# One identity for all stages, last stores moved between queues, last keys turned from features, and weights waited for one by one

## The reference

```python
xp = layer_norm(x_prompt, ln_in_g, ln_in_b)              # xs likewise for the 64 sample rows
q, k, v, z, xbc, dt_raw, u, vc = split_cols(x @ w_in, IN_SIZES)
o_a = band_attention_prompt(q, k, v, attn_rel_bias)      # 6 heads x 64, a band of 9 chunks of 64
k_rows, v_rows = k[:, L - keep:], v[:, L - keep:]        # returned: the last 512 keys and values
...                                                      # (sample: attention on cache_k, cache_v; 64 new keys)
o_b, ssm_conv_state, ssm_h = mamba_mixer(z, xbc, dt_raw, ...)   # 6 heads x 64, chunked scan over 128 rows
o_c = chunk_mlp(gelu(u), gelu(vc), gmlp_w, gmlp_b)
mixed = concat([rms_norm(o_a), rms_norm(o_b), rms_norm(o_c)])
x = layer_norm(DN_ALPHA * x + mixed @ w_out, ln1_g, ln1_b)
up, ffn_conv_state = causal_dwconv(x @ ffn_w_in, ffn_conv_prev, ffn_conv_w, ffn_conv_b)
gate, val = split_cols(up, (D_FF, D_FF))                 # D_FF = 2816
x = layer_norm(DN_ALPHA * x + (silu(gate) * val) @ ffn_w_out, ln2_g, ln2_b)
```

## Time and profile before

| | |
|---|---|
| median of 3 runs | 2680.27 us (2678.9 to 2684.03) |
| the profiled execution | 2686.66 us, its span 2685.2 us |
| mean granted TensorE clock | 0.978 of full speed |
| TensorE, weight loads | 95%, 88% busy |
| VectorE, ScalarE, GpSimd | 60%, 40%, 8% busy |
| DMA | 471 MB, mean 175 GB/s |

### The profile page before, as it was taken

The page is one execution under the profiler, slowest core; times in us unless marked ns, Lnnn a source line. Parts: engine busy times, 40 slices in busy tenths (PEclk is TensorE's granted clock), DMA queues, the critical chain, the costliest instruction groups (busy, mean ns, idle before and its releaser), DMA issues. The chain is left out here.

```text
span 2685.2 us, 46989 instructions
## 1 busy us (share of the span) xinstructions
PE 2555.4 (95%) x15072; PEld 2352.2 (88%) x15072; DVE 1620.2 (60%) x3171; ACT 1086.0 (40%) x2144; POOL 204.7 (8%) x286
## 2 busy tenths in 40 slices
PE   6999899999999889988999899999999999999998
PEld 5888799998998868868999899999999977888885
DVE  5433456457785667768999966668666653333332
ACT  4454422226563542325555544445445441111110
POOL 0001100011013741110000000000000000000000
PEclk9999999998997989999999999999999999999999
DMA  5446434235553734638777888887888753232221
GB/s 194 154 137 206 145 124 155 79 105 131 134 131 111 232 130 166 225 125 279 253 245 242 268 267 257 259 256 239 252 253 258 237 192 113 80 87 88 80 78 52
DMA packets 404522, 471.10 MB, mean 175 GB/s; under 512 B 39466, under 2 KB 337180, under 8 KB 404402
## 3 DMA queue, kind: packets, MB, share of 16 engines
q1 hardware_dynamic: 384722, 406.83, 48.6%
q0 software_dynamic: 19696, 62.94, 7.3%
HBM read 315.00 MB, written 157.57 MB: 176 GB/s over the span
## 5 line engine op out<-in xcount | busy, mean ns | idle before, releaser
L2728 PE MATMUL fu_ps_a<-mo_fu_x_hi,mo_fu_w 128*128 128x354 f32 (+1 forms) x1056 | 347.0, 329 | 27.0 <-DVE fu_c L2691 10.4
L2730 PE MATMUL fu_ps_a<-mo_fu_x_hi,mo_fu_w 128*128 128x354 f32 (+1 forms) x1056 | 344.5, 326 | 0.0
L119 PE MATMUL fd_ps_y<-fu_fd_w,fu_fd_h_hi 128*128 128x512 f32 (+1 forms) x748 | 292.3, 391 | 7.0 <-PEq L2159 6.3
L120 PE MATMUL fd_ps_y<-fu_fd_w,fu_fd_h_hi 128*128 128x512 f32 (+1 forms) x748 | 291.7, 390 | 0.0
L121 PE MATMUL fd_ps_y<-fu_fd_w,fu_fd_h_lo 128*128 128x512 f32 (+1 forms) x748 | 291.5, 390 | 0.0
L2919 DVE TENSOR_TENSOR fu_fd_h_lo<-fu_fd_h_raw,fu_fd_h_hi 128x256 fp32r<-128x256 f32 (+1 forms) x185 | 76.9, 416 | 309.8 <-ACT fu_fd_h_hi L2889 309.7
L2729 PE MATMUL fu_ps_a<-fu_x_lo_rest,mo_fu_w 128*128 128x354 f32 (+1 forms) x792 | 257.2, 325 | 0.0
L2889 ACT CAST fu_fd_h_hi<-fu_fd_h_raw 128x256 fp32r<-128x256 f32 (+1 forms) x185 | 74.0, 401 | 403.3 <-PE fd_ps_y L121 392.6
L2728 PEld LDWEIGHTS fu_ps_a<-mo_fu_x_hi,mo_fu_w 128*128 128x128 f32 x1056 | 200.2, 190 | 35.9 <-DVE mo_fu_w L2601 11.8
L2730 PEld LDWEIGHTS fu_ps_a<-mo_fu_x_hi,mo_fu_w 128*128 128x128 f32 x1056 | 200.0, 189 | 0.0
L2728 PE MATMUL fu_ps_c<-mo_fu_x_hi,mo_fu_w 128*128 128x354 f32 (+1 forms) x528 | 171.9, 326 | 8.8 <-ACT fu_part L2523 8.8
(11 more groups left out here) (416 smaller groups left out, 6285.2 us busy)
## 6 DMA issues: line engine op xcount, KB each, us to landing
mo_fu_w<-fu_w_split SPq DMA_DIRECT2D x176, 512.0 KB, 4.5
fu_w_raw<-ffn_w_in SPq DMA_DIRECT2D x131, 512.0 KB, 5.8
fu_w_split<-mo_fu_w SPq DMA_DIRECT2D x44, 1024.0 KB, 5.9
fu_fd_h_raw<-h_t SPq DMA_DIRECT2D x176, 128.0 KB, 2.2
h_t<-fu_val SPq DMA_DIRECT2D x88, 176.0 KB, 1.9
fu_fd_raw<-ffn_w_out SPq DMA_DIRECT2D x22, 512.0 KB, 4.4
x_rows<-pr_xr SPq DMA_DIRECT2D x16, 512.0 KB, 2.8
xt<-pr_xt SPq DMA_DIRECT2D x16, 512.0 KB, 4.0
```

The lines of the kernel that those rows point to most:

```text
L119: pe.matmul(out, lhs_hi, rhs_hi, start=first, stop=False)
L120: pe.matmul(out, lhs_hi, rhs_lo, start=False, stop=False)
L2728: pe.matmul(out, wh, xh, start=first and k == 0, stop=False, skip_group_check=True)
L2730: last = pe.matmul(out, wl, xh, start=False, stop=k == KH - 1, skip_group_check=True)
```

## The change

1. One identity, made in `project_rows` at a fixed place (`IDENT_AT`); the others are gone, with their waits.
2. SyncE no longer waits for its stores at the end of pr and pf. The waits stand at the start of the next stage: on GpSimd ahead of its first loads in pf, and on SyncE, GpSimd and VectorE in at (`landed`).
3. `turn_keys` moves from tile 16 to tile 4 and is made from the stored features: GpSimd loads both parts in tile 1 (128x3x576 float32 each), VectorE adds them in tile 3 (3 additions of 128x576), TensorE transposes 3 pieces in each of heads 0 to 4 of tile 4, ScalarE copies, and SyncE stores at the start of its step for tile 5, ahead of the load of tile 6.
4. The last stores of at, sg, mo and fd go from GpSimd to SyncE; the two state stores of fu go from SyncE to ScalarE.
5. `w_out`: a semaphore each for pieces 0 to 3, one for the last four; ScalarE waits in each chunk only for what it splits.
6. `dta_parts`, `upper` and its rounded copy are made during attention (tile 16, and GpSimd's `load_constants`).

The core of the diff:

```diff
-    ident = m.sb("ident", [P, P])
+    ident = d["ident"]                                   # pf, at, sg, mo, fu; made once in pr
-                make_identity(pool, ident, zero_done, ident_done)      # pf, at, sg, mo, fu
-                pe.wait_ge(ident_done, 1)
...
 # project_rows, SyncE, end
-                for p, count in ((0, 9), (1, 8)):
-                    sp.wait_ge(xr_stored[p], 16 * count)
-                    sp.wait_ge(xt_stored[p], 16 * count)
-                    sp.wait_ge(y_stored[p], 64 * count)
 # project_features, GpSimd, start
+                for p, count in ((0, 9), (1, 8)):
+                    pool.wait_ge(d["pr_stored"]["xr_stored"][p], 16 * count)
+                    pool.wait_ge(d["pr_stored"]["xt_stored"][p], 16 * count)
+                    pool.wait_ge(d["pr_stored"]["y_stored"][p], 64 * count)
...
 # attention, SyncE
+                    if isinstance(cur.t, int) and cur.t == LOOP0 - 1:
+                        sp.wait_ge(rows_done, 5)
+                        sp.dma_start(d["prompt_k"].rearrange("(b p) w -> p b w", p=P), k_rows[:, 0:4, :]).then_inc(rows_stored, 16)
+                        sp.dma_start(d["sample_k"], k_rows[:NSMP, 4, :]).then_inc(rows_stored, 16)
...
-                sp.wait_ge(rows_done, 5)
-                sp.dma_start(d["prompt_k"].rearrange("(b p) w -> p b w", p=P), k_rows[:, 0:4, :]).then_inc(rows_stored, 16)
-                sp.dma_start(d["sample_k"], k_rows[:NSMP, 4, :]).then_inc(rows_stored, 16)
+                sp.wait_ge(o_done, HEADS * (NT + 1))
+                sp.dma_start(d["mixed"][tile_rows(NT), 0:AW], o[:last.nq, 0, :]).then_inc(sg["smp_stored"], 16)
 # attention, GpSimd
+                    if isinstance(cur.t, int) and cur.t == 1:
+                        for e, part in enumerate(("qk_hi", "qk_lo")):
+                            pool.dma_start(k_t[:, e], d[part][AW:, SEQ - CACHE:].rearrange("(c p) r -> p c r", p=P)).then_inc(keys_loaded, 16)
...
-                store_o(Band(NT), 0)
 # attention, VectorE
+                    if isinstance(b.t, int) and b.t == LOOP0 - 3 and h < AW // P:
+                        dve.wait_ge(keys_loaded, 32)
+                        dve.tensor_tensor(k_t[:, 0, h], k_t[:, 0, h], k_t[:, 1, h], ALU.add).then_inc(keys_summed, 1)
 # attention, ScalarE
+                    if turns_keys(b, h):
+                        n = P if h < 4 else NSMP
+                        act.wait_ge(rows_turned, h + 1)
+                        act.copy(k_rows[:n, h, :], ps_o[:n, h % 2, 0:AW]).then_inc(rows_done, 1)
 # attention, TensorE
+                def turn_keys(b, h):
+                    n = P if h < 4 else NSMP
+                    if h == 0:
+                        pe.wait_ge(keys_summed, AW // P)
+                    pe.wait_ge(o_done, HEADS * b.t + h - 1)
+                    for c in range(AW // P):
+                        last = pe.transpose(ps_o[:n, h % 2, c * P:(c + 1) * P], k_t[:, 0, c, h * P:h * P + n], ident[:])
+                    last.then_inc(rows_turned, 1)
...
 # ssd_and_gmlp, ScalarE
                     if 12 <= t < NT:
-                        act.wait_ge(mo["w_loaded"], 16 * KD)
                         for k in (2 * (t - 12), 2 * (t - 12) + 1):
+                            if k < 4:
+                                act.wait_ge(mo["w_loaded"][k], 16)
+                            else:
+                                act.wait_ge(mo["w_late"], 16 * 4)
                             act.copy(mo["w_hi"][:, k, :], mo["w_raw"][:, k, :]).then_inc(mo["w_hi_done"], 1)
 # ssd_and_gmlp, end: from GpSimd to SyncE
+                sp.wait_ge(fin_done, 2)
+                for f, name in enumerate(("prompt_ssm", "sample_ssm")):
+                    sp.dma_start(d[name].rearrange("(m p) n -> p m n", p=P), st_out[:, f]).then_inc(fin_stored, 16)
...
 # mix_out, SyncE, end (GpSimd leaves it out)
+                sp.wait_ge(yt_done, NT)
+                sp.dma_start(d["x1t"][:, :, tile_rows(NT - 1)], yt[:, 1]).then_inc(smp_stored, 16)
...
 # ffn_down, end: from GpSimd to SyncE
+                sp.wait_ge(y_done, NT + 1)
+                sp.dma_start(d["y_sample"], y[:NSMP, 0, :]).then_inc(smp_stored, 16)
+                sp.wait_ge(smp_stored, 16)
+                sp.wait_ge(y_stored[0], 16 * 8)
+                sp.wait_ge(y_stored[1], 16 * 8)
```

More of the change, by code:

```diff
@@ L135, in project_rows @@
                   for name in ("dt", "dta", "ncum", "ecum", "dts", "etot")}
+    d["ident"] = nc.alloc_sbuf_tensor_at("ident", [P, P], F32, offset=IDENT_AT)
+    stored = {name: [nc.alloc_semaphore(f"pr_{name}{i}") for i in range(2)] for name in ("xr_stored", "xt_stored", "y_stored")}
+    d["pr_stored"] = stored
     with nc.cleanup_on_exit(), ExitStack() as ctx:
@@ L933, in attention @@
         cache = m.sb("cache", [P, 4, HEADS, 2, HD])
-        ident, ident_r = m.sb("ident", [P, P]), m.sb("ident_r", [P, HD], F32R)
+        ident = d["ident"]
+        sg["upper"], sg["upper_r"] = m.sb("sg_upper", [P, P]), m.sb("sg_upper_r", [P, P], F32R)
+        sg["dta_parts"] = m.sb("sg_dta_parts", [P, NT + 1, 2 * HEADS], F32R)
         s = m.sb("s", [P, 3, WIN])
@@ L939, in attention @@
         k_rows = m.sb("k_rows", [P, 5, AW])
+        k_t = m.over("k_t", m.here(), [P, 2, AW // P, CACHE + NSMP])
         for name, shape in (("xbc", [P, 2, NXBC, P]), ("z", [P, 2, AW]), ("uv", [P, 2, 2 * CW])):
@@ L1040, in turned_keys, with turns_keys, landed @@
             return ps_o[:, i % 2, 0:2 * P].rearrange("p (b c) -> p b c", c=P)
-        def key_rows(b, n):
-            return ps_s[:n, b // 2, (b % 2) * 512:(b % 2) * 512 + AW] if b < 4 else ps_t[:n, 0:AW]
+        def turns_keys(b, h):
+            return isinstance(b.t, int) and b.t == LOOP0 - 2 and h < 5
+        def landed(eng):
+            for done, count in zip(d["pf_stored"].values(), d["pf_counts"]):
+                eng.wait_ge(done, count)
         with nc.Block() as block:
@@ L1102, in load_constants @@
                     pool.wait_ge(cache_turned, 2 * HEADS)
+                    pool.memset(sg["upper"][:], 1.0).then_inc(one_done, 1)
+                    pool.wait_ge(one_done, 1)
+                    pool.affine_select(out=sg["upper"][:], in_=sg["upper"][:], compare_op=ALU.is_ge, fill=0.0, base=0,
+                                       pattern=[[1, P]], channel_multiplier=-1).then_inc(upper_done, 1)
                     pool.dma_start(sg["d_row"][:, 0:HEADS], bc_row(d["ssm_d"], HEADS)).then_inc(next_loaded, 16)
@@ L1224, in step @@
                         act.copy(keys(0, i // 2, cache_blocks(i)), turned_keys(i)).then_inc(cache_hi_done, 1)
+                    if turns_keys(b, h):
+                        n = P if h < 4 else NSMP
+                        act.wait_ge(rows_turned, h + 1)
+                        act.copy(k_rows[:n, h, :], ps_o[:n, h % 2, 0:AW]).then_inc(rows_done, 1)
+                    if isinstance(b.t, int) and b.t == NT and h == 0:
+                        act.copy(sg["dta_parts"][:, :, 0:HEADS], d["steps"]["dta"][:]).then_inc(dta_hi_done, 1)
+                    if isinstance(b.t, int) and b.t == NT and h == HEADS - 1:
+                        act.wait_ge(upper_done, 1)
+                        act.copy(sg["upper_r"][:], sg["upper"][:])
                 heads(act, step)
@@ L1353, in ssd_and_gmlp @@
         st_out, ob, oc = m.sb("st_out", [P, 2, 3, P]), m.sb("ob", [P, 2, AW]), m.sb("oc", [P, 2, CW])
-        ident, upper, ones = m.sb("ident", [P, P]), m.sb("upper", [P, P]), m.sb("ones", [P, P])
+        ident = d["ident"]
         dt, dta, ncum, ecum, dts, etot = (d["steps"][name] for name in ("dt", "dta", "ncum", "ecum", "dts", "etot"))
         head = d["sg"]
-        d_row, ws, gb, st_in = (head[name] for name in ("d_row", "ws", "gb", "st_in"))
+        d_row, ws, gb, st_in, upper, upper_r, dta_parts = (head[name] for name in ("d_row", "ws", "gb", "st_in", "upper", "upper_r", "dta_parts"))
         d_row = d_row[:, 0:HEADS]
@@ L1594, in _ @@
             def _(dve):
-                dve.wait_ge(dta_hi_done, 1)
-                dve.tensor_tensor(dta_parts[:, :, HEADS:], dta[:], dta_parts[:, :, 0:HEADS].bitcast(F32), ALU.subtract).then_inc(dta_lo_done, 1)
                 dve.memset(state[:], 0.0).then_inc(state_done, 1)
@@ L1927, in step @@
                         pool.dma_start(d["x1_rows"][tile_rows(t), :], y[:n, p, :]).then_inc(y_stored[p], 16)
-                    if not (isinstance(t, int) and t == 0):
+                    if not (isinstance(t, int) and t in (0, NT)):
                         store_yt(t - 1, 1 - p)
```

149 lines of the change are left out of this document (47 added, 102 removed).

## The result

The changed kernel takes 2661.2 us (median of 4 runs, 2658.4 to 2664.5) against 2681.0: a ratio of 0.9926, with a 95% interval of 0.9909 to 0.9943, 15 to 24 us less. Run again beside other executions of before it took 2662.0 against 2683.9, ratio 0.9906 (0.9889 to 0.9924). The forecast was 2648.6, its range 2640 to 2657: the gain is real, and some two thirds of what was said.

A forecast was written before the change was run, and what follows sets the result against it. TensorE, busy for 95% of the span, was taken to bound the kernel. Gains of 35.8 us less 4.1 added gave 31.7 less, from the median 2680.27 to 2648.6 us; range 2640 to 2657, 8 in 10.

The forecast's parts named there:

- Ends of stages, 9.7: At six stage ends, dropped waits for stores and stores moved off GpSimd or SyncE shorten the end: 9.7 us less together.
- the forecast's own terms, 972.0 and two issues of 0.6 and 0.37: Scan's end: from 972.0, two SyncE issues and its DRAIN end at 973.4 in place of GpSimd's 975.56: 2.2 us less.
- the 1.0 taken for it: End of ffn_down: issue and landing of `y_sample` on SyncE together get shorter by 1.0 us (0 to 1.5).
- mix_out's 1.2: End of mix_out: with GpSimd's last store on SyncE, whose own end stays, 1.2 us less.
- Identity and start of the scan, 2.8: Starts of mix_out and scan: TensorE no longer waits for the identity (1.5 us less) or for `upper` (1.3 less).
- End of attention, 14.1: End of attention: without `turn_keys` and with the last store on SyncE, 14.4 us less, net 14.1 after small added steps.
- the rival in which it returns sooner: Start of the scan: half clock of at most 16 us becomes 8 or less, 3 to 6 us more gained, 2644; 12%.
- Chunk 12, 9.2: Scan, chunk 12: ScalarE's wait for the last `w_out` piece goes (4.1 us), and half clock after it (5.1): 9.2 less.
- The first rival (the clock falls anyway): Near chunk 12 of the scan the clock still falls, only 4.1 of 9.2 us comes: 2653.7; 12%.
- Added work, 4.1: Attention: VectorE's additions in tile 3 (1.0), transposes in tile 4 (1.6), key stores ahead of tile 6's load (1.5): 4.1 us more.
- The rival "loads collide": Attention, tiles 3 to 7: tile 6 or 7 waits for its load behind the key stores, 5 to 8 us more, 2655; 13%.
- 35.8 less: Sum of all gains over the whole kernel, before the added work: 9.7 + 1.5 + 1.3 + 14.1 + 9.2 us.

The follow-up runs named there:

- the experiment: The changed kernel with the last stores of attention, scan, mix_out and ffn_down issued by GpSimd again: 2666.62 us, 4.7 more, ratio 0.9934.

## Why the prediction was wrong

The direction and most terms held; one term was wrong in kind.

* **Ends of stages, 9.7.** Nearly right in size: 7.8 to 9.0. By the traces pr gave 1.7, the pf end and the identity of attention 1.5, the scan 2.1 (the forecast's own terms, 972.0 and two issues of 0.6 and 0.37, end at 973.6 and not at 973.4, so they give 2.0), ffn_up 0.8, ffn_down 1.7 (the landing after SyncE's issue took nearly as long as before, so the 1.0 taken for it was 0.3). mix_out's 1.2 did not show when undone: GpSimd's DRAIN there varies from 4.2 to 5.4 us, and in the second execution of before it ended only 0.03 us after SyncE's. That SyncE's DRAIN is short behind a store of its own is shown: 0.37 us in three stages. On GpSimd it took 3757, 4031 and 4221 ns in the experiment. The Trainium skill's 12 ns ("VectorE: DVE Perf Modes", The DRAIN you can't avoid), which it gives for the boilerplate DRAINs, don't describe these block ends.
* **Identity and start of the scan, 2.8.** The waits are gone: TensorE starts 0.04 and 0.19 us after SyncE in the scan and in mix_out. mix_out as a whole gained only 1.2 of 2.7. Its second round of transposes comes 1.7 us sooner after the stage's start than before (15.9 us against 17.7), behind a wait of 2.1 us for VectorE that both kernels have. Behind this wait both executions of the changed kernel have some 3 us at half clock, and both of before have none (the row below is the changed kernel's). Of the other executions whose start and end of mix_out are the changed kernel's, three have such a stretch and took 228.0 to 228.2 us; four have none and took 226.9 to 227.9, which is 1.5 to 2.5 less than before. So the clock hides a part of the term, and what decides whether it falls there is not known:

```profile
974.00:976.00 2.00, 2.00 (x6) 1.59 (x5) 1.56 (x5) 0.94 (x2) 0.00 (x0) 0.50 0.78 272
```

* **End of attention, 14.1.** Right: 14.1. The half clock that the forecast left as it was lasted 16.3 us into the scan in both executions (17.7 and 9.8 before), so the rival in which it returns sooner did not come.
* **Chunk 12, 9.2.** Right: 9.5 in time, 9.5 to 9.8 in the scan's length when undone. The first rival (the clock falls anyway) is out.
* **Added work, 4.1.** This is the step that failed: it came to 13.6. Its parts on the engines were right: tile 3 took 0.8 more (1.0 forecast), tile 4 1.2 (1.6). The loads of the features were called hidden; they landed in time for the additions, in 5.9 and 8.9 us, but tile 3's queries, issued behind them, came 1.4 us late for TensorE. And "the two key stores stand in SyncE's queue ahead of tile 6's load ... 1.5 (0 to 4)" was 9.5 to 10.3. I priced the bytes ahead of the load. What the stores bring is their wait: SyncE could not issue the load before ScalarE's fifth copy and the two stores, so it began 4.7 us later within its tile than before, 3.7 of them for the wait. That put the load into the cache copies, the next load with it, and TensorE stood for 3.0 us. The rival "loads collide" named the place and priced it at 5 to 8 more, without what follows a standstill of that length: half clock through most of tile 7, which cost 7.1 us, over twice the wait itself. In chunk 12 I had read the same pair, a wait of 4 and then 5 at half clock, and did not carry it over.

The sum with the right term: 35.8 less, 1.6 and 0.8 and 1.2 and 10 more, is 22 less, and the two medians have 20 and 22. That it fits so closely is in part luck: mix_out gave 1.5 less than its terms, and ffn_up came out 2.8 shorter than the change explains.

The best kernel of the runs is the changed one with the key stores in tile 15: 2650.9 us, 1.3% below before and 0.4% below the changed kernel. Behind the load of tile 6 they do as well.

## What to carry to other kernels

Where a store is put ahead of a load in a queue, ask not how many bytes go first but what the store waits for: all loads behind it inherit that wait, and one load that leaves its slot can meet a burst it used to miss. Price a standstill of TensorE together with the clock after it; here 3 us of waiting cost 10 in most executions, and 3 to 4 where the clock held or soon came back. When work is moved from a stage's end into its steady part, the end gave here what its timeline showed, and the steady part must be checked tile by tile for who is now ahead of whom.

## What was not expected of the hardware

* A standstill of 3.0 us (2.2 in the second execution) in tile 6 was followed by half clock for 13 us or more, with TensorE busy throughout; in the kernel with one wait for all weights a wait of 2.6 us was followed by a tile 7 of only 14.9, with 3.4 us at half clock, and in the one with the later loads a wait of 2.8 us by none. So neither whether the clock falls nor for how long follows from the length of the wait. A row from the changed kernel:

```profile
683.00:696.50 13.50, 13.50 (x61) 12.92 (x60) 5.88 (x22) 4.46 (x11) 0.55 (x1) 0.50 0.11 28
```

* A DRAIN of GpSimd right behind its own store took 3.6 to 5.4 us, and one of SyncE 0.37; behind a store that had landed they took 1.45 us and 7 ns.
* SyncE's issue of a single 192 KB load took 5.08 us in the crowded stretch (3.45 with the stores behind the load), where others take 0.4 to 0.6 (3.65 in the kernel before, too): the issue itself can be held up, and with it all that follows in the queue.
